# One step of a hybrid decoder trunk: decode products on VectorE and ScalarE instead of GpSimd, and four other parts of the order moved

## The reference

```
xn = rmsnorm(x, g_mix);  proj = xn @ w_in + b_in            # conv gates, q, k, v, o, two head gates
y_conv = gb * short_conv(gc * hc, state_conv, conv_w)       # width 512, 3 taps
h, (C, n, m) = mlstm(q, k, v, ig, lf, C0, n0, m0)           # 4 heads of 128, with a running maximum
x = x + concat(y_conv, sigmoid(o) * rmsnorm(h) * g_mh) @ w_out
mk, mv = split(rmsnorm(mem, g_mem) @ w_xkv)                 # 256 memory rows, prompt only
s = softmax(q(x) . mk / sqrt(256));  x = x + (s . mv) @ w_xo   # 4 heads of 256; decode tokens: own cache
g, u = split(rmsnorm(x, g_ffn) @ w_gu)
x = x + (silu(g) * u) @ w_down                              # 1024 -> 2 * 2816 -> 1024
y = rmsnorm(x, g_final)
```

## Time and profile before

| | |
|---|---|
| median of three runs | 2924.15 us (2921.01 to 2927.12) |
| profiled execution | 2919.49 us, span 2917.6 us |
| granted TensorE clock, mean | 0.985 |
| busy | TensorE 2810.0, VectorE 1592.6, ScalarE 1079.4, GpSimd 839.8 us |
| feed-forward begins | 1472.07 us, after a wait of 3.64 us |
| last block of it begins | 2423.79 us, after a wait of 3.61 us |

### The profile page before, as it was taken

The page is one execution under the profiler, slowest core; times in us unless marked ns, Lnnn a source line. Parts: engine busy times, 40 slices in busy tenths (PEclk is TensorE's granted clock), DMA queues, the critical chain, the costliest instruction groups (busy, mean ns, idle before and its releaser), DMA issues. The chain is left out here.

```text
span 2917.6 us, 42678 instructions
## 1 busy us (share of the span) xinstructions
PE 2810.0 (96%) x16543; PEld 2688.6 (92%) x16543; DVE 1592.6 (55%) x2834; ACT 1079.4 (37%) x2133; POOL 839.8 (29%) x781
## 2 busy tenths in 40 slices
PE   8889999999999999999999999999999999999997
PEld 8778879999998998999889999999999999999997
DVE  7635654346445446545485556575555559455654
ACT  6433343233223322322253334353442345333432
POOL 2633431002400185285022222222221222222221
PEclk9999999999999999999999999999999999999998
DMA  7977758767956888798732212234221232322222
GB/s 267 323 292 265 284 187 309 264 257 278 385 212 259 336 317 310 262 359 305 258 110 97 80 62 77 86 105 150 87 75 57 87 126 83 111 86 62 76 80 68
DMA packets 163023, 546.73 MB, mean 187 GB/s; under 512 B 17452, under 2 KB 71916, under 8 KB 126600
## 3 DMA queue, kind: packets, MB, share of 16 engines
q1 hardware_dynamic: 144192, 490.25, 46.6%
q0 software_dynamic: 9232, 42.05, 4.2%
q10 hardware_dynamic: 9400, 11.72, 1.2%
HBM read 450.09 MB, written 93.87 MB: 186 GB/s over the span
## 5 line engine op out<-in xcount | busy, mean ns | idle before, releaser
L874 POOL TENSOR_TENSOR units<-wq,units 128x512 fp32r<-128x512 f32 (+1 forms) x276 | 362.3, 1323 | 1130.2 <-ACT units L1406 1129.9
L914 PE MATMUL gb<-xn_hi,w_hl 128*128 128x384 f32 (+2 forms) x2280 | 649.1, 356 | 3.0 <-DVE big L1844 2.6
L914 PEld LDWEIGHTS gb<-xn_hi,w_hl 128*128 128x128 f32 x2280 | 422.0, 189 | 24.3 <-issue 3.9
L1296 PE MATMUL gb<-tq,units 128*128 128x342 f32 (+1 forms) x2772 | 439.9, 319 | 0.0
L1296 PEld LDWEIGHTS gb<-tq,units 128*128 128x128 f32 x2772 | 435.7, 188 | 0.0
L1406 ACT ACTIVATE units<-wq 128x512 fp32r<-128x512 f32 (+1 forms) x540 | 319.1, 614 | 273.4 <-DVE wq L1921 195.3
L914 PE MATMUL gb<-xn_lo,w_hl 128*128 128x384 f32 (+2 forms) x1160 | 408.1, 352 | 0.0
L914 PE MATMUL gb<-act_hi,w_hl 128*128 128x384 f32 (+3 forms) x1424 | 379.9, 345 | 14.7 <-DVE w_hl L1813 10.3
L914 PEld LDWEIGHTS gb<-act_hi,w_hl 128*128 128x128 f32 x1424 | 260.4, 191 | 30.1 <-DVE w_hl L1813 10.6
L1296 PE MATMUL gm<-tq,units 128*128 128x342 f32 (+1 forms) x1584 | 275.2, 323 | 13.4 <-DVE tq L1954 10.9
L1296 PEld LDWEIGHTS gm<-tq,units 128*128 128x128 f32 x1584 | 256.2, 191 | 15.9 <-issue 12.1
(11 more groups left out here) (360 smaller groups left out, 4168.7 us busy)
## 6 DMA issues: line engine op xcount, KB each, us to landing
w_hl<-split_d SPq DMA_DIRECT2D x212, 1024.0 KB, 7.2
wq<-w_gu SPq DMA_DIRECT2D x132, 512.0 KB, 4.3
split_d<-w_hl SPq DMA_DIRECT2D x53, 1024.0 KB, 5.9
wq<-w_dn SPq DMA_DIRECT2D x120, 256.0 KB, 2.9
w_raw<-w_st SPq DMA_DIRECT2D x37, 512.0 KB, 6.8
w_raw<-w_kv SPq DMA_DIRECT2D x32, 512.0 KB, 5.5
made_d<-big ACTq DMA_DIRECT2D x32, 256.0 KB, 3.8
w_raw<-made_d SPq DMA_DIRECT2D x16, 512.0 KB, 7.0
```

What stands on the lines that cost most here:

```text
L874: pool.tensor_tensor(units[:, u % NU, 1, 0:w], unit_source(u), units[:, u % NU, 0, 0:w].bitcast(F32), ALU.subtract).then_inc(unit_lo_p, 1)
L914: mm = pe.matmul(bank[:, 0:wd], a[:, s, k * P:(k + 1) * P], r[:, k, 0:wd], start=(first and k == ks[0] and i == 0), stop=(last and k == ks ...
L1296: mm = pe.matmul(bank[:, 0:n], units[:, u % NU, a, k * P:(k + 1) * P], tq[:, t, r, k, 0:n], start=(p in (0, 1, 3) and k == 0 and i == 0), ...
```

## The change

**Decode (block 2, 3, 4).** The products leave GpSimd, which keeps only the transfers and now waits for `state_done`, `piece_mul` and `piece_sum` before it reuses a buffer. The states become five steps a head on VectorE (`dec_state`), placed in head h for head h+1 (head 0's at the start of block 2, behind `dec_conv`). A piece becomes one multiplication on VectorE (`piece`) and four `Copy` activations with an accumulated total on ScalarE (`piece_total`). `PIECE_HEAD` puts three pieces into each of heads 1 to 3 of block 3 and four into each head of block 4; `PIECE_OUT` puts one behind each of output tiles 0 to 6 of block 3.

**First rows.** For block 0, GpSimd issues the four broadcast loads behind its low half of weight tile `O_HEAD + 3` (`bc_first`).

**Feed-forward operands.** The top-right quarter now is loaded into a spare part of `T_T2`, and `T_T4` is made. Loads, differences (`made_operand`), highs and lows are spread anew: for block 0 two loads at `O_OUT + 7` and one difference and one low ahead of the scores; for the others the first difference behind the last pair, the others in down tiles 1 and 2, lows in tiles 0 and 3 to 7.

**Residual halves.** The final scales stand in the places of `SCALE_AT`; `y_stored` and `xf_loaded` are two semaphores each, one for tiles 0 to 3 and one for 4 to 7, and the load of the first half is issued at unit `2 * size` instead of `2 * size + 3`.

**Last group.** The sixteen down products of the very last group go by column halves: all eight tiles of half 0, then all of half 1 (`last_down`). Half 0 is summed behind the third tile of half 1 (`sum_half`), and its scales and stores go between the rest.

The core of the diff:

```diff
-MADE_AT = {T_T1: 1, T_T2: 2, T_T3: 3, T_T4: 4}
-LOAD_AT = {T_B11: 0, T_B21: 1, T_B22: 2, T_T4: 3}
+HIGH_ORDER = [T_B11, T_T1, T_B21, T_T2, T_T3, T_B22, T_T4]
+LOAD_AT = {T_B11: 0, T_B21: 2, T_B22: 3}
+L_B12 = 1
+MADE_AT = {T_T1: 1, T_T3: 2, T_T2: 3, T_T4: 4}
+SCALE_AT = [(1, 0), (1, 2), (1, 3), (1, 4), (1, 6), (2, 0), (2, 2), (2, 3)]
+PIECE_HEAD, PIECE_OUT = {}, {}
+for _h in range(1, HEADS):
+    PIECE_HEAD[DO + 1, _h] = list(range(3 * _h - 3, 3 * _h))
+for _e in range(7):
+    PIECE_OUT[DO + 1, _e] = [9 + _e]
+for _h in range(HEADS):
+    PIECE_HEAD[DX, _h] = list(range(16 + 4 * _h, 20 + 4 * _h))
...
@@ SyncE @@
-                elif off == 17:
-                    all_made(sp)
-                    load_rows(0)
...
-                        if gr == 0 and i == 2 * size + 1:
+                        if gr == 0 and i == 2 * size:
                             if b:
                                 sp.wait_ge(y_ready, 8 * b)
                                 store_y(b - 1, 4)
+                                sp.wait_ge(y_stored[0], 32 * b)
+                                load_xf(b, 0)
...
-                        if gr == 0 and i == 2 * size + 3:
+                        if gr == 0 and i == 2 * size + 1:
                             if b:
-                                sp.wait_ge(y_stored, 64 * b)
+                                sp.wait_ge(y_stored[1], 32 * b)
...
-                            load_xf(b, 0)
+                                load_xf(b, 0)
                             load_xf(b, 4)
                         if gr == NG - 1 and b < NFB - 1 and i == 2 * size + 2:
-                            sp.wait_ge(product_done, last_product(b, 1))
+                            sp.wait_ge(product_done, last_product(b, 2))
                             operand(b + 1, 0)
+                            operand(b + 1, 2)
                             operand(b + 1, 1)
...
@@ GpSimd @@
+                if g == gw(0, O_HEAD + 3):
+                    n = tok(0) + BLK[0]
+                    all_made(pool)
+                    pool.wait_ge(rows_stored, 32)
+                    for h in range(HEADS):
+                        pool.dma_start(bc[:, h, 0:n], rows_d[h:h + 1, 0:n].to_broadcast([P, n])).then_inc(bc_first, 16)
...
-            for i in range(NROW):
-                piece_row(i)
             for i in range(4 * NDEC):
...
-                piece(i)
-                n = i + NROW
-                if n < 4 * NDEC and not 2 * NDEC <= n < 2 * NDEC + NROW:
-                    piece_row(n)
-                if i % 2 and i // 2 + 2 < 2 * NDEC:
-                    cache(i // 2 + 2)
+                piece_row(i)
+                if i % 2 == 0 and 4 <= i:
+                    cache(i // 2)
...
@@ ScalarE @@
+            def piece_total(i):
+                t, j = (i // 2) % NDEC, i % 2
+                c = i // 2
+                act.wait_ge(piece_mul, i + 1)
+                for n in range(4):
...
+                        part, total = dcache[:, c % 2, a:a + 256], dy[:, o:o + 1]
+                    ins = act.activation(part, part, ACT.Copy, accum_out=total)
+                ins.then_inc(piece_sum, 1)
...
                     act.activation(yc[:, 0:TOK], ub[:, 0:TOK], ACT.Copy, scale=col(C_CW + 3 * h)).then_inc(tap_done, 1)
+                    for i in PIECE_HEAD.get((b, h), ()):
+                        piece_total(i)
...
                     res_tile(g, e, 0, C_GCROSS, W)
+                    for i in PIECE_OUT.get((b, e), ()):
+                        piece_total(i)
...
@@ TensorE, the last group: tile(i, ks) writes last_bank(i) from units of m = i % 8 and ah of half i // 8 @@
+                for i in range(2, 2 * KT):
+                    if i < KT:
+                        unit_ready(unit_at(b, gr, -1, i))
+                    after(pe, evac_done, d + i - 3 if i > 3 else 0)
+                    tile(i, range(size))
+                    if i == KT + 2:
+                        sum_half(b, 0)
+                sum_half(b, 1)
...
@@ VectorE @@
+            def dec_state(h, i):
+                c_h, k = c_dec[:, h * NDEC:(h + 1) * NDEC, :], h * NDEC
+                if i == 0:
...
+                    st(v.tensor_tensor(k_bc, k_bc, vv, ALU.mult))
+                elif i < 3:
...
+                    for t in range(4 * i - 4, 4 * i):
+                        a = v.scalar_tensor_tensor(out=c_h[:, t, :], in0=c_h[:, t, :], scalar=dbc[:, h, t:t + 1], in1=k_bc[:, t, :],
+                                                   op0=ALU.mult, op1=ALU.add)
...
+                elif i == 3:
...
+                    st(v.tensor_tensor(q_bc, q_bc, c_h, ALU.mult))
+                else:
...
+                    v.tensor_reduce(dnum[:, k:k + NDEC], q_bc, AX.X, ALU.add).then_inc(state_done, 1)
+            def piece(i):
...
+                v.wait_ge(cache_loaded[c % 2], 16 * (c // 2) + 16)
+                v.wait_ge(row_loaded[i % NROW], 16 * (i // NROW) + 16)
...
+                    v.tensor_tensor(part, part, row, ALU.mult).then_inc(piece_mul, 1)
...
+                    for i in PIECE_HEAD.get((b, h), ())[:2]:
+                        piece(i)
                     wv(0)
...
                     both(0)
+                    if b == DO and h < HEADS - 1:
+                        dec_state(h + 1, 2)
+                    for i in PIECE_HEAD.get((b, h), ())[2:3]:
+                        piece(i)
...
                     both(1)
+                    if b == DO and h < HEADS - 1:
+                        dec_state(h + 1, 3)
+                    for i in PIECE_HEAD.get((b, h), ())[3:]:
+                        piece(i)
...
                     res_tile(gw(b, O_OUT + e), e, 0, C_GCROSS, W)
+                    for i in PIECE_OUT.get((b, e), ()):
+                        piece(i)
...
-                            for i in {4: (0, 1), 5: (2, 3)}.get(p, ()):
-                                made_operand(b + 1, i)
-                            for i in {6: (0, 1), 7: (2, 3)}.get(p, ()):
-                                operand_low(b + 1, i)
-                if gr == 0 and f == 0 and p < 3:
-                    operand_low(b, p + 4)
+                        for t in {1: (T_T3, T_T2), 2: (T_T4,)}.get(p, ()):
+                            made_operand(b + 1, t)
+                        for i in {0: (0,), 3: (1,), 4: (2,), 5: (3,), 6: (4,), 7: (5,)}.get(p, ()):
+                            operand_low(b + 1, i)
+                if gr == 0 and f == 0 and p < (1 if b else 3):
+                    operand_low(b, p + (6 if b else 4))
```

366 lines of the change are left out of this document (217 added, 149 removed).

## The result

The changed kernel has a median of 2873.19 us (2869.98 to 2877.76, four runs) beside 2923.31 us of the kernel before on the same chip (four runs). The ratio is 0.9828 with a 95% interval of 0.981 to 0.9847, so 50 us or 1.7% less. The forecast was 2863.8 in a range of 2847 to 2889: the sign and the order of size held, and the gain was 10 us smaller than forecast. The profiled execution has a span of 2867.5 us, 50.1 less than before, and a mean clock of 0.994.

What follows compares the result with a forecast made beforehand. TensorE, busy 2810 of 2917.6 us, was taken as the bound, so time could come only from its waits, slow clock, start and end. Terms A to F summed to -60.4 us, giving 2863.8 in a range of 2847 to 2889.

Steps and rivals of the forecast that it cites:

- A: First head: gate rows loaded on GpSimd's queue instead of SP's remove the 10.0 us wait and slow clock, -11.9 us.
- C: Feed-forward entry: moving operand loads, one difference and one low half earlier removes waits and slow clock, -7.2 us.
- D: Group 0 of each block: earlier scales and residual halves bring the down weights sooner, removing three waits, -18 us.
- F: Tail after the last down product: column halves put half the sums, scales and stores under the last tiles, -8.8 us.
- B in the heads: Blocks 2 to 4: decode off GpSimd ends seven waits and two slow stretches, -18.8 us, plus 5 for tight heads and late caches.
- rivals 1 and 4: Block 3 outputs, heads at upper bounds, E nothing: 2885, 0.27 with two others; decode pieces clock every head: 2941, 0.03.
- B in block 3: Block 3's output tiles: a VectorE and ScalarE chain of 4.4 us a tile causes two waits of 3.1 us, +8.5 us.
- E: Two block boundaries: differences and six lows moved into the down phase, -4.6 us each, -9.2 together.
- Rival 3: Feed-forward waits only move: down weights still behind the residual (D -6), E 0; 2885 us, chance 0.27 with two other rivals.

Runs made afterwards that it cites:

- Experiment 1: Changed kernel with block 0's broadcast gate rows issued again by SP behind its weight loads, not by GpSimd; one execution 2879.91 us.
- experiment 11: Changed kernel with four pieces in each of heads 1 to 3 of block 3, four behind output tiles 2 to 5, sums one tile later; one execution 2863.37 us.
- Experiments 10: Changed kernel with ScalarE's four sums of a piece one output tile later in block 3; the stage won only 1.3 us.
- experiment 7: Changed kernel with the old feed-forward entry: all four operand loads late, no difference or low half ahead of the scores; 2874.39 us, ratio 0.983.
- (9): Changed kernel with ScalarE's sixteen sums of block 4's last head ahead of its squares; six rows issued 6 us sooner, wait 3.4 us for 3.8.
- (8): Changed kernel with the first half of the decode output products one output tile earlier in block 4; shift 0.2 us over the stage.
- experiment 6: Changed kernel with both block boundaries as they were (operand loads, differences, high and low halves); 2873.85 us, ratio 0.9829.
- experiment 4: Changed kernel with the partition sums of the block before two products later in the next block's first pair; shift -0.5 and -1.1 us.

## Why the prediction was right, and where it was not

- **The sum came nearer than its terms.** The forecast missed by 10 us, but the heads gave 8.8 us more than forecast while the weight rows took 5.5 that no term had, so these two misses partly cancel. Only A and the boundaries were tested by undoing them, C in part. For D, F and the heads the cause rests on the waits and stretched operations that are gone from the trace, and on the order of the two programs.
- **A and F were right in size**, -12.0 for -11.9 and -9.4 for -8.8 (F's own terms add up to -8.9). Experiment 1 shows A's cause. A's margin was thinner than its working: the last of the four rows took 11.1 us to land, not 6.8, and there was just enough slack.
- **B in the heads was right in mechanism and too careful in size.** Not one 128x3 operation is stretched and no head waits: the 5 us that I had set aside for tight heads and late caches weren't needed, and 22.6 came where 18.8 was the sum. 1.6 of the difference is a stretch of low clock at 849 us that happened not to come, which is luck. One reading was off: beside the 2.59 ran a piece's multiplication (GpSimd, 1099.74 to 1102.12), not a fold; both left GpSimd with the change. The heads bear four pieces each (experiment 11), so rivals 1 and 4 have no ground there.
- **B in block 3 was right**: 4.45 us a tile for 4.4, 7.7 for 8.5, though the pair of waits of 3 us came as 3.21 and 1.52. Experiments 10 and 11 add what the prediction lacked: behind the chain stood a second bound, since a cache tile is asked for only by the sum of a piece that is itself in this stage.
- **B's weight rows were missed.** No term had them: 3.8 us of wait and its slow stretch, 5.5 in all. Its cause isn't settled. The moved operand loads alone are not it (7), nor is the later issue of the first six rows alone (9), and starting earlier moves the wait (8). That these two act together, as the two causes at the boundary did, wasn't tried; the weights on the way (4 MB, and 3 MB in either experiment, for 2 MB before) would fit that, but don't show it.
- **C was mis-sized**: "I leave 0.6 of it all". The wait for the operand and the slow clock went, but those for a weight operand and for `c`, 1.7 and 0.8, are there as before, to within 0.01. I take them to hang on the weights' chain of the first pair and not on the operand's delay, which no run shows. The 4.9 us themselves are read from one pair of traces; experiment 7 gave back 2.7.
- **D was right**: -16.1 for -18. The first group keeps a wait of 1.1 us, and the recovered clock was less than counted.
- **E failed**, and with it most of the missing 10 us. The step is "One more wait of 0.7 comes where operand loads stand ahead of the down weights", with "1.2 for small waits behind" as a gain. The wait was 2.90 and 2.27, because two delays meet on the hidden low half: SP's queue, which I had, and VectorE's own queue, in which the difference had been put ahead of it, which I hadn't. The small waits didn't go. The sums waited 1.9 for the 2.7 I gave them. A stretch of low clock came back in each boundary, 0.66 in the mean over 1925 to 1930 and over 2362 to 2367, which the sum left out and only its bound of 0 had: 1.7 each by the prediction's own price. That makes -0.3 and -0.9 of the -4.6; the 1.5 and 0.5 that are left I can't place. The differences, priced at 1.5 each, took up to 2.67 beside GpSimd, which the sum didn't have either. What was forecast as -4.6 each came out as +1.2 and -0.4, and experiment 6 agrees in the time. Rival 3 had said it: the boundary's wait goes elsewhere, E is 0. Its other half, the down weights still behind the residual in group 0, didn't come.

## What to carry to other kernels

Where an instruction is put into an in-order queue, price its own duration for everything behind it, and its wait too: the difference ahead of the low half cost as much as the transfer that I had counted. When a late tile has two causes, taking one away shows little; try them together before calling either innocent. And two traces with the same matmuls can be subtracted, start by start: that gives each edit's worth with its clock, more finely than timed runs can, if stretches of low clock that come by chance are told apart.

## What the runs showed of the hardware

The same wait doesn't always cost the same clock. At one matmul, at 849 us in the kernel before and at 834 to 846 in the other traces, TensorE waits 2.48 or 2.49 us in every trace. In 11 of the 14 traces the granted clock then falls to its lower level for 3.4 us, which the shift shows as 1.6 us; in three, the changed kernel's among them, it stays at 2.4 GHz. It can also cost more: behind the waits of 3.21 and 1.52 us at block 3's scores the mean clock over 11 us was 0.84 in the changed kernel (1120 to 1131), but 0.54 behind waits of 2.94 and 1.52 in experiment 4 (1122 to 1133) and 0.53 in experiment 7, for 2.0 and 1.7 us more by the shift. So the price of 1.7 behind a wait is a typical value, neither fixed nor a bound.

While GpSimd multiplied in SBUF, a VectorE operation on 128x3 took 2.59 us in place of 0.17; with GpSimd silent none exceeds 0.18. That agrees with the exclusive port of the Trainium skill (page "SBUF — State Buffer", section "SBUF: two separate sides"). It holds for large operations too: a difference of 128x1368 took 1.58 us alone and 2.66 beside GpSimd's low halves. The section's other sentence, on transfers issued by GpSimd that starve, can't be read from these runs: the last gate row landed in 11.1 us and the last weight row in 11.5, where such loads took 6.8 in the median and 5.9 in the kernel before, but in the second case the transfers of all queues together ran at 360 to 490 GB/s throughout.
